# Two-layer hybrid decoder trunk in split FP32 matmuls: strip 0's gate product moved into strip 1, the down projection opened with one token half of four rows, quad transposes put behind the next chunk

## The reference

```python
def swiglu(h, w_gate, w_up, w_down):
    return (jax.nn.silu(h @ w_gate) * (h @ w_up)) @ w_down

def memory_cross_attention(h, mem_n, wq, wk, wv, wo):
    q = (h @ wq).reshape(B, S, X_HEADS, X_HEAD_DIM)
    k = (mem_n @ wk).reshape(B, M, X_HEADS, X_HEAD_DIM)
    v = (mem_n @ wv).reshape(B, M, X_HEADS, X_HEAD_DIM)
    ...
```

## Time and profile before

| | |
|---|---|
| median of three runs | 3076.94 us |
| the profiled execution's own time | 3080.78 us |
| its span in the profile | 3078.9 us |
| TensorE busy, matmuls | 2940.4 us (96%) |
| VectorE busy | 1837.8 us (60%) |
| ScalarE busy | 1438.5 us (47%) |
| mean granted TensorE clock | 0.981 of full |
| HBM read | 560.41 MB, 187 GB/s over the span |

### The profile page before, as it was taken

How to read it: one execution, slowest core, us unless ns; L and a number is a source line. 1 busy time by engine, 2 the same in 40 slices (tenths; PEclk the granted TensorE clock), 3 DMA queues, 4 the chain that set the end, 5 groups by cost and what they waited for, 6 DMA issues and landing times.

```text
span 3078.9 us, 35720 instructions
## 1 busy us (share of the span) xinstructions
PE 2940.4 (96%) x13262; PEld 2431.8 (79%) x13262; DVE 1837.8 (60%) x1537; ACT 1438.5 (47%) x1548; POOL 97.7 (3%) x109
## 2 busy tenths in 40 slices
PE   6999999999998999999998999999999899999998
PEld 5888878887786888887887878777787788887887
DVE  5444444446446888885555536555446888886554
ACT  4343344434334666554444434444334556665443
POOL 0000000001001000000002000001001000000000
PEclk9999999999999999999999979999999999999999
DMA  7665656465345655556554625565436455665553
GB/s 264 210 218 188 212 191 191 150 219 178 123 164 191 218 188 186 185 206 228 194 191 150 190 75 180 193 231 178 164 130 215 152 187 218 219 219 178 191 193 134
DMA packets 254175, 576.90 MB, mean 187 GB/s; under 512 B 14176, under 2 KB 14192, under 8 KB 250080
## 3 DMA queue, kind: packets, MB, share of 16 engines
q1 hardware_dynamic: 249376, 530.63, 50.5%
q0 software_dynamic: 3504, 31.92, 2.6%
q10 hardware_dynamic: 1168, 12.59, 1.1%
HBM read 560.41 MB, written 14.68 MB: 187 GB/s over the span
## 4 chain that ended last, share of the span: by engine, by line
PE 90%; DVE 4%; issue 2%; POOL 1%; ACT 1%; DMA 1%; DVEq 0%; SPq 0%; POOLq 0%; ACTq 0%
PE ps L1505 88%; POOL w_lo L437 1%; DVE w_lo L974 1%; DMA w_raw<-in_xattn_wk 1%; PE ps L1575 1%; PE ps L1589 1%; PE ps L1842 1%; DVE xres L1089 0%; ACT w_hi L551 0%; DVE w_lo L1397 0%; DVE y L1085 0%; ACT ps L640 0%; DVE gb L1265 0%; DVE act_lo L1020 0%; DVE wide L1401 0%
## 5 line engine op out<-in xcount | busy, mean ns | idle before, releaser
L1505 PE MATMUL ps<-w_hi,act_hi 128*128 128x512 f32 x3632 | 1340.3, 393 | 44.3 <-DVE act_lo L1020 23.0
L1505 PE MATMUL ps<-w_lo,act_hi 128*128 128x512 f32 x3632 | 1334.7, 391 | 0.0
L1505 PE MATMUL ps<-w_hi,act_lo 128*128 128x512 f32 x3632 | 1333.7, 391 | 0.0
L974 DVE TENSOR_TENSOR w_lo<-w_raw,w_hi 128x1024 fp32r<-128x1024 f32 x673 | 796.2, 1222 | 594.4 <-ACT w_hi L551 591.2
L551 ACT ACTIVATE w_hi<-w_raw 128x1024 fp32r<-128x1024 f32 x688 | 694.1, 1051 | 647.3 <-PE ps L1505 527.7
L1505 PEld LDWEIGHTS ps<-w_hi,act_hi 128*128 128x128 f32 x3632 | 686.3, 189 | 191.9 <-issue 40.5
L1505 PEld LDWEIGHTS ps<-w_hi,act_lo 128*128 128x128 f32 x3632 | 685.7, 189 | 144.0
L1505 PEld LDWEIGHTS ps<-w_lo,act_hi 128*128 128x128 f32 x3632 | 686.5, 189 | 142.0 <-issue 0.2
L1397 DVE TENSOR_TENSOR w_lo<-wide,w_hi 128x2048 fp32r<-128x2048 f32 x180 | 410.5, 2288 | 66.1 <-ACT w_hi L876 65.6
L876 ACT ACTIVATE w_hi<-wide 128x2048 fp32r<-128x2048 f32 x180 | 344.2, 1913 | 160.9 <-PE ps L1505 104.5
L946 ACT ACTIVATE act_hi<-mid 128x256 fp32r x80 | 33.4, 418 | 259.7 <-PE ps L1505 259.7
(11 more groups left out here) (185 smaller groups left out, 1308.8 us busy)
## 6 DMA issues: line engine op xcount, KB each, us to landing
w_raw<-in_ffn_w_down SPq DMA_DIRECT2D x176, 512.0 KB, 4.1
wide<-in_ffn_w_gate SPq DMA_DIRECT2D x80, 1024.0 KB, 10.3
wide<-in_ffn_w_up SPq DMA_DIRECT2D x80, 1024.0 KB, 8.9
w_raw<-in_odd_w_in SPq DMA_DIRECT2D x96, 512.0 KB, 4.5
w_raw<-in_xattn_wk SPq DMA_DIRECT2D x64, 512.0 KB, 4.7
w_raw<-in_xattn_wv SPq DMA_DIRECT2D x64, 512.0 KB, 4.4
w_raw<-in_even_w_in SPq DMA_DIRECT2D x64, 512.0 KB, 4.5
w_raw<-in_xattn_wq SPq DMA_DIRECT2D x64, 512.0 KB, 4.6
```

Of the source, the lines that this page charges most:

```text
L974: nc.vector.tensor_tensor(w_lo[:, at_slot, part], w_raw[:, (2 * s + h) % RAW_SLOTS, :], w_hi[:, at_slot, part].bitcast(F32), ALU.subtract)\
L1505: return nc.tensor.matmul(dst, lhs, rhs, start=start, stop=stop, skip_group_check=loose)
```

## The change

It has three parts.

1. VectorE's `times_up` for strip 0 stands inside strip 1, behind low part 2 (the third), in the place where `gather` stands in the later strips.
2. The down projection's first four activation blocks are made right behind the last strip (ScalarE as soon as that strip's product 0 has released `act_hi`). TensorE runs token half 0 of rows 0 to 3, then the last strip's transposes, then waits for `mid_taken`, then token half 1 of rows 0 to 3. The four slots are released in that second half.
3. The transposes of a projection's second quad stand behind the first chunk of the third quad. Those of the fourth quad are returned by `transposed`: for `mk0` and `mk1` they are put behind the first chunk of `mv0` and `mv1`; for `sb_qk`, `gla_qk` and `xq` they are issued at once, as before. TensorE's four loops (`mk1`, `mv0`, `mv1`, `gla_v`) are written out.

```diff
@@ scalar
+                act.wait_ge(w_used, summed(l, STRIPS - 1)[0] + 1 + W_SLOTS)
+                for s in range(4):
+                    nc.scalar.activation(act_hi[:, s, :], mid[:, s, :], ACT.Copy).then_inc(jit_hi, 1)
                 split(ck, 0)
                 split(ck, 1)
                 silu(STRIPS - 1)
...
-                act.wait_ge(w_used, pl["c"] + W_SLOTS)
-                for s in range(4):
-                    nc.scalar.activation(act_hi[:, s, :], mid[:, s, :], ACT.Copy).then_inc(jit_hi, 1)
@@ vector, strip
                     if i > 1:
                         gather(i - 1)
+                    else:
+                        times_up()
                     wide_lo(c, 3, at[B21])
...
-                times_up()
                 for i in range(1, STRIPS):
                     strip(i)
+                jit0 = l * FT
+                for s in range(4):
+                    dve.wait_ge(jit_hi, jit0 + s + 1)
+                    nc.vector.tensor_tensor(act_lo[:, s, :], mid[:, s, :], act_hi[:, s, :].bitcast(F32),
+                                            ALU.subtract).then_inc(jit_done, 1)
@@ tensor, transposed
-                def second(i):
-                    quad(chunks(pl, i), i + (pl["u"] + 1), 1, lambda: transpose_quad(i, pl, 0))
-                    transpose_quad(i, pl, 1)
                 if source is None:
-                    with pe.Fori(0, 2) as i:
-                        quad(chunks(pl, i), i + (pl["u"] + 1), 0)
-                        second(i)
+                    quad(chunks(pl, 0), pl["u"] + 1, 0)
                 else:
                     opening(name, source, h_done, 2 * NORMS.index(source))
-                    second(0)
-                    quad(chunks(pl, add=8), 1 + (pl["u"] + 1), 0)
-                    second(1)
+                quad(chunks(pl, 0), pl["u"] + 1, 1, lambda: transpose_quad(0, pl, 0))
+                quad(chunks(pl, 1), pl["u"] + 2, 0, lambda: transpose_quad(0, pl, 1))
+                quad(chunks(pl, 1), pl["u"] + 2, 1, lambda: transpose_quad(1, pl, 0))
+                return lambda: transpose_quad(1, pl, 1)
...
+            def natural(name, pairs=(0, 1), after_first=None):
...
+                        quad(chunks(pl, i), i + (pl["u"] + 1), q, after_first if i + q == 0 else None)
...
-                transposed(f"mk{l}", "mem_norm" if l == 0 else None)
-                natural(f"mv{l}")
+                rest = transposed(f"mk{l}", "mem_norm" if l == 0 else None)
+                natural(f"mv{l}", after_first=rest)
...
-                    transposed("sb_qk", "pre_mix0")
+                    transposed("sb_qk", "pre_mix0")()
@@ tensor, down
-                transpose_mid(STRIPS - 1)
...
+                for s in range(4):
+                    row_ready(0, s)
+                    row(s, 0, s == 0)
+                transpose_mid(STRIPS - 1)
                 pe.wait_ge(mid_taken, STRIPS * (l + 1))
                 for s in range(4):
-                    row_ready(0, s)
-                    for m in range(MT):
-                        last = row(s, m, s == 0)
-                    last.then_inc(w_used, 1)
+                    row(s, 1, s == 0).then_inc(w_used, 1)
```

More of the change, by code:

```diff
@@ L929, in _ @@
                     strip(i)
-                pl, ck = plan[f"down{l}"], chunks(plan[f"down{l}"])
+                act.wait_ge(w_used, summed(l, STRIPS - 1)[0] + 1 + W_SLOTS)
+                for s in range(4):
+                    nc.scalar.activation(act_hi[:, s, :], mid[:, s, :], ACT.Copy).then_inc(jit_hi, 1)
+                ck = chunks(plan[f"down{l}"])
                 split(ck, 0)
                 split(ck, 1)
-                pl = plan[f"gu{l}"]
                 silu(STRIPS - 1)
@@ L1466, in _ @@
                 pl = plan[f"down{l}"]
-                jit0 = l * FT
                 def jit(i, s):
@@ L1474, in jit @@
                         .then_inc(jit_done, 1)
[L1475 to L1478, removed]
                 def rows(i):
@@ L1605, in transposed @@
                 pl = plan[name]
-                def second(i):
-                    quad(chunks(pl, i), i + (pl["u"] + 1), 1, lambda: transpose_quad(i, pl, 0))
-                    transpose_quad(i, pl, 1)
                 if source is None:
-                    with pe.Fori(0, 2) as i:
-                        quad(chunks(pl, i), i + (pl["u"] + 1), 0)
-                        second(i)
+                    quad(chunks(pl, 0), pl["u"] + 1, 0)
                 else:
                     opening(name, source, h_done, 2 * NORMS.index(source))
-                    second(0)
-                    quad(chunks(pl, add=8), 1 + (pl["u"] + 1), 0)
-                    second(1)
-            def natural(name, pairs=None):
+                quad(chunks(pl, 0), pl["u"] + 1, 1, lambda: transpose_quad(0, pl, 0))
[3 more added lines that the diff above has]
+            def natural(name, pairs=(0, 1), after_first=None):
                 pl = plan[name]
-                def one(i):
+                for i in pairs:
                     for q in range(2):
[L1625 to L1631, removed]
+                        quad(chunks(pl, i), i + (pl["u"] + 1), q, after_first if i + q == 0 else None)
             def output(name, opened=False):
@@ L1720, in _ @@
                 else:
-                    transposed("gla_qk", "pre_mix1")
+                    transposed("gla_qk", "pre_mix1")()
                     pl = plan["gla_a"]
@@ L1789, in _ @@
                 output(f"mix_out{l}", opened=l == 1)
-                transposed(f"xq{l}", f"pre_x{l}")
+                transposed(f"xq{l}", f"pre_x{l}")()
                 pl = plan[f"x_s{l}"]
@@ L1827, in _ @@
                 pl = plan[f"gu{l}"]
+                pu = pl
                 def transpose_mid(i):
@@ L1831, in transpose_mid @@
                         if i == 0:
-                            pe.wait_ge(bank_free[2 + m], pl["u"] + 2)
+                            pe.wait_ge(bank_free[2 + m], pu["u"] + 2)
                         else:
@@ L1839, in transpose_mid @@
                         if i == 0:
-                            emptied(b, pl)
+                            emptied(b, pu)
                         for m in range(MT):
```

## The result

| | before | changed |
| --- | --- | --- |
| median of the timed runs, us | 3079.12 (4 runs, 3076.62 to 3081.62) | 3044.46 (4 runs, 3043.21 to 3044.93) |
| ratio of the two, 95% interval | | 0.9881 [0.9868, 0.9893] |
| profiled execution: own time / span, us | 3080.78 / 3078.9 | 3044.26 / 3042.4 |
| mean granted clock of TensorE | 0.981 | 0.984 |

The changed kernel is 1.2% faster. The forecast was 3038.5 us, range 3031 to 3048: the sign, the size and the range hold, and the point is 6.0 us low. Of these, 2.2 us are the base: the three runs of before that were shown had their median at 3076.94, the four of this comparison at 3079.12, and 25 runs on another occasion at 3079.43. The other 3.8 us are gain that was forecast (38.5) and did not come (34.7 between the medians, 36.5 between the profiled executions).

A forecast was written before the change was run, and what follows sets the result against it. TensorE, busy 96% of the span, bounds the kernel; what can be won is its waits and low clock. Gains of 19.2 + 11.1 + 8.2 = 38.5 us give 3042.3, less 3.84 for the median: 3038.5 us, range 3031 to 3048.

The forecast's parts named there:

- Price of undisturbed work: TensorE's chain that ended last: 504 matmuls in 114.29 us, 0.2268 us each; stretches are measured against it.
- Part 1: Opening of strip 1: product 1 waits about 2.1 us for the gate product; gains 10.3 and 8.95, together 19.2 us.
- 2.02 us nearer: Strip 1, layer 1: VectorE starts 2.02 us nearer to its matmuls' end, so product 1 starts at 2396.2.
- Part 2: Opening of down: new loss 2.7 us against 8.59 and 7.94, from waits for bank 3 and `mid`; 11.1 us gained.
- Part 3: Quad transposes: eight of twelve places moved, each saving 1.02 us, 8.2 us in all; nothing waits.
- Loops: TensorE's four written-out loops: no work added, and nothing counted for their branches.
- Sum: Whole kernel: 19.2 + 11.1 + 8.2 = 38.5 us off the profiled execution's 3080.78, giving 3042.3.
- From there to the median: The median of the runs lies 3.84 us below the profiled execution, so 3042.3 becomes 3038.5 us.
- Rival 1: TensorE's clock falls at the four new waits at strip 1 and down, costing 16 us: 3054.5 us; chance 0.10.
- The argument from the earlier trace: At 719 to 724 us TensorE idled 2.14 us in one piece at clock 1.00, which speaks against a falling clock.
- Rival 2: More comes free than counted, at strip 1's remaining losses or the branches: 6 us more, 3032.5; chance 0.11.
- Rivals 3 and 4: Late copies at quad transposes starve weight loads: 3096 us, 0.02; one part, likeliest down's, does nothing: 3044.6 us, 0.08.

The follow-up runs named there:

- early kernel: Changed kernel with strip 0's gate product (`times_up`) behind low part 1 in place of low part 2: 3037.79 us, ratio 0.9866.
- the loops alone: Kernel before with only TensorE's four loops (`mk1`, `mv0`, `mv1`, `gla_v`) written out, transposes where they were: 3081.15 us, ratio 1.0003.
- part 1 alone: Kernel before with only strip 0's gate product moved behind low part 2: 3063.55 us, ratio 0.9947.
- second trace of the changed kernel: Changed kernel, unchanged, profiled once more: span 3045.7 us, 3.3 more than in its first trace.
- doubled delay: Changed kernel with the moved quad transposes behind the second chunk of the next quad instead of the first (second-chunk kernel): 3041.33 us, ratio 0.9879.
- part 2 alone: Kernel before with only down's opening changed: early activation blocks, token half 0, transposes, token half 1: 3072.63 us, ratio 0.9976.
- down edit: Changed kernel with down's row 0 going bank by bank and the last strip's transposes behind row 2 instead of row 3: 3037.92 us, ratio 0.9867.
- late kernel: Changed kernel with strip 0's gate product one place later, behind low part 3: 3052.74 us, ratio 0.9914.

## Why the prediction was right, step by step

- **Price of undisturbed work** (0.2268 us per matmul): held. With the waits gone, the early kernel's stretches come to -0.01 and 0.09 us of it.
- **Part 1: 10.3 + 8.95 = 19.2.** Measured 10.4 + 9.2 = 19.6. The order of VectorE, low part 0 ahead of the end of strip 0, the release of product 1 by the gate product: all as written. The forecast wait was 2.1 us, the trace shows 1.83 of idleness and 2.12 lost. Layer 1 was put at 2.35 by its shorter lead; it lost 2.09. (The "2.02 us nearer" of that sentence is a slip: by the rows named there the lead is 0.14 us shorter, and the start at 2396.2 goes by that.)
- **Part 2: 11.1**, a new loss of 2.7 per layer. Measured 10.6, a loss of 2.98. The waits came as named, 1.09 us for bank 3 (1.0 forecast) and 1.20 for `mid`. The term that was mis-sized is the one for the copy and the restarts: 1.5 + 0.2 forecast, about 1.9 measured (2.98 less 1.09).
- **Part 3: 8 x 1.02 = 8.2.** Measured 8.1. Four waits of 0.83 stay, as said. The chunk times behind the transposes were not measured one by one; no new wait shows there.
- **Loops: nothing.** Measured nothing, with the loops alone.
- **Sum: 38.5** against the profiled execution; the places show 38.3. The step that failed is the silent one, that the rest of the kernel keeps its time. Against the profiled execution 3042.3 was forecast and 3044.26 measured: 0.2 us from the terms, 1.8 from elsewhere. That this is only 1.8 is partly luck: three new low stretches cost 5.9 us, and 3.3 of them are hidden by two that only the first trace of before had.
- **From there to the median: 3.84 us less**, by the three runs shown. That was weaker than it was taken to be: in the larger sets before stands at 3079.4 to 3080.9, and the changed kernel's median lies 0.2 us above its profiled execution. A scatter of 5 us in three runs was passed on as an offset of the kernel. Counted this way, 4.0 of the 6.0 us by which the point is low come from this step and 2.0 from the one above.
- **Rival 1** was given 0.10 as four falls of the clock together. It exists as a chance at strip 1: 1.7 us, seen at one of two places in part 1 alone and at one of two in the second trace of the changed kernel. Of ten such waits (1.2 to 2.0 us, in five traces) two were followed by a low stretch, and the longest was not. At down's waits, 1.1 to 1.3 us, no trace shows one. The argument from the earlier trace rows, one stretch with 2.14 us of idleness at clock 1.00, was one instance of a thing that goes both ways.
- **Rival 2** (less loss at strip 1 than counted) did not come by itself, but the early kernel shows that the loss was avoidable: 4.1 of the 6 us. **Rivals 3 and 4**: refuted, by the doubled delay and by part 2 alone.

## What to carry to other kernels

Where one engine is busy for 96% of the span, list its idle gaps, ask for each which instruction stands at the head of the releasing engine's queue, and whether that one is wanted soonest; here three re-orderings with no work removed gave 1.2%, and moving the gate product by one more low part, ordering down's first row by bank and putting the transposes one row earlier gave another 0.3 to 0.4%. Put a step behind the last thing that is wanted before it, and count both sides: one low part too late cost 2.1 us a layer, two cost 6.0. Small gains are read at their own place, instruction by instruction, since the span of one and the same kernel moves from one execution to the next (before: 3074.8 to 3080.9 us in 25 runs). Then look at the rest as well, at the same matmuls in two traces of each kernel: what is new and returns in both is not scatter.

## What the runs showed of the hardware

- TensorE's granted clock fell to 0.50 behind an idle wait of 1.94 us (part 1 alone, layer 0) and of 1.84 us (changed kernel, second trace), and stayed at 1.00 behind one of 1.83 us (changed kernel, first trace, same instruction). Behind a wait of 2.00 us (the down edit, layer 0) it stayed at 1.00 as well, so the length of the wait alone does not decide. Behind the late kernel's waits of 4.17 and 4.01 us it fell in both layers. I had taken 2.1 us for short enough.
- One and the same kernel spends 118.0 or 127.8 us at the low level, in two executions; the changed one 97.8 or 101.4. The Trainium skill (TensorE: Matmul & The Clock Gate, Part 1) says that the number of slow matmuls at a kernel's start varies from run to run of the same kernel; the traces here agree (the second of before has a low stretch at 23 us, the first has none) and show the same for some of the low stretches in the middle.
- The wait for the low part that opens `gla_v` (L973) is 0.9 us in before and 1.9 in the changed kernel, in both traces of each within 0.1, and between 0.4 and 1.9 in the others, with no order that follows the edits. The loops alone leave it at 1.0. In both traces of the changed kernel a low stretch follows it, so the place costs 2.6 us more than in before; behind nearly the same wait (1.9 and 1.8 us) in the second-chunk and the early kernel none follows. Its cause stays open.
- One low stretch, at the transposes of L1589 that follow layer 0, is in all eight traces of kernels with part 2 and in none of the five without, for 1.6 us, some 260 us behind the place of the edit. How the two hang together is not shown.
